# Two transposed token tiles in two pairs of banks, a first gated chunk cut by token tile, and a weight split moved between two additions

## The chip, the cores and the metric

One core of a Trainium2 chip runs one program; everything is fp32 in and out. The metric is the device time of one execution in microseconds, lower is better. Matmuls run on the tensor engine (TensorE, PE) and write to PSUM; VectorE (DVE), ScalarE (ACT) and GpSimd (POOL) do the rest, SyncE (SP) starts the weight loads.

## What is computed

Two transformer blocks, one behind the other, on one sequence of 256 tokens of 1024 features. The change touches the first:

```python
def first_block(x, ...):
    for i in range(DEPTH):                      # 2 layers
        h = rms_norm(x, ln_attn_g[i])
        dq, dk, dv, mq, mk, mv = jnp.split(h @ w_in[i], cuts, axis=-1)
        ...                                     # two kinds of attention, causal
        x = x + jnp.concatenate([y_diff, y_moba], axis=-1) @ w_out[i]
        x = x + conv_ffn(rms_norm(x, ln_ffn_g[i]), w_up[i], conv_w[i], conv_b[i], w_down[i])
    return x

def conv_ffn(h, w_up, conv_w, conv_b, w_down):
    u = causal_dwconv(h @ w_up, conv_w, conv_b)
    g, up = jnp.split(u, 2, axis=-1)            # 2816 features each
    return (jax.nn.silu(g) * up) @ w_down
```

The second block (modulated norms, a recurrent mixer, three more attentions, squared-relu MLPs) begins with norms of a context (`mix_ctx`) and of the stream (`mix_lat`), whose products (`projA`) follow the last `down1`.

## The kernel before

**Products.** Each large product is a sum of three rounded (single-pass) matmuls per k-tile of 128: the operands are split into a rounded high half and a rounded rest, and `mm3` (L401 to L403) multiplies high by high, high by low and low by high. Weights come in chunks of 128 x 2048 numbers (1 MB), loaded by SyncE into 4 raw slots. ScalarE writes a chunk's high half (`ahead_act`, L374), VectorE subtracts it in place (`ahead_dve`, L385, "the split"). Both work in chunk order up to HIGH = 3 chunks ahead of the product. A token product (`tok_gemm`: `qkv`, `out1`, `down1`) keeps 128 tokens as the stationary side and moves 512 weight columns; it works in blocks of 512 columns, in each in pieces of 4 k-tiles, in each piece first token tile 0, then tile 1. `out1` has 2 pieces a block, `down1` 6, of which the last has 2 k-tiles. The gated product (`up1_pe`, L1353) is by features: the stationary side is a tile of 128 weight columns, the moving side all 256 tokens, in 22 chunks; each fills one accumulation bank with 2 (gate and up) x 256 tokens, in 2 x 8 x 3 = 48 matmuls.

**Banks.** PSUM has 8 banks: 4 `acc`, 2 `tr` for transposes, 2 `sc` for scores. Every fill has a number within its pool, fixed ahead by `stage`; `claim` waits until the bank's former fill has been drained, `filled` until the fill is there, `drain` counts a drained one.

**The residual and the norm.** Both products that end a half layer are added to the stream by VectorE in `add_dve` (L1338): for each block of 512 columns the splits that fall due, then the additions of token tile 0 and tile 1 (L1345), then the last split. Then the norm follows, by 128-token tile: ScalarE squares and sums (`norm_square`, L582), GpSimd adds epsilon and takes the power -0.5 (L589, L591), VectorE scales the tile (`norm_scale`, L602), TensorE transposes it in two halves of 4 blocks of 128x128 (`norm_turn`, L611), ScalarE writes the rounded high half with the gain (`norm_high`, L638), VectorE the low half (`norm_low`, L656). The norms with a shift (second block) use L628, L634, L648 and L653 in their place. `norm_dve` (L659) sets VectorE's order: scale tile 0, low half of tile 0's first half, scale tile 1, the other three low halves. Both tiles' four halves go through the 2 `tr` banks, so tile 1's transposes wait until tile 0's banks are drained.

**What follows the norms.** `qkv_pe` (attention, layer 1) starts with tile 0's first half, turns tile 1 after 12 matmuls, and takes tile 0's second half before tile 1. `up1_pe` waits in its first chunk for both tiles' halves (L1361, `norm_ready` L673). After the last `down1` `projA_pe` starts with the context and turns the stream's tiles after its first and second feature tile (L725), so the stream's norm is wanted later there.

The order of work on each engine is the order in which the code is written; nothing reorders it.

Of the kernel before, what the change touches and what calls it, by code (L numbers as in the profile page):

```python
# [11 lines left out]
ALU = mybir.AluOpType  # L12
# [115 lines left out]
def first_and_second_block(nc, I, consts, out):  # L128

    with ExitStack() as ctx:  # L130
# [279 lines left out]
        norm_n = {}  # L410

        def plan_norm(key):
            norm_n[key] = len(norm_n)
            stage(("norm", key), tr=4)

# [157 lines left out]
        def norm_fill(key, tt, half):  # L573

            return tr_at[("norm", key)] + 2 * tt + half

# [16 lines left out]
        def norm_scale(dve, norm, tt):  # L593

            key, src, ready, gain, shift, dst = norm
            n = norm_tile(key, tt)
            ready(dve, tt)
            if norm_n[key]:
                before = [k for k in norm_n if norm_n[k] == norm_n[key] - 1][0]
                dve.wait_ge(tr_full, norm_fill(before, tt, 1) + 1)  # L600
            dve.wait_ge(norm_rstd, n + 1)
            dve.tensor_scalar(xn[:, tt, :], src[:, tt, :], norm_rs[:, n:n + 1], None, ALU.mult).then_inc(norm_xn, 1)  # L602

        def norm_turn(pe, key, tt):

            pe.wait_ge(norm_xn, norm_tile(key, tt) + 1)
            for half in range(2):
                ps = claim(pe, "tr", norm_fill(key, tt, half))
# [3 lines left out]
                ins.then_inc(tr_full, 1)  # L612

# [7 lines left out]
        def norm_high(act, norm, tt):  # L621

            key, src, ready, gain, shift, dst = norm
            if shift:
                f, hi, lo, cols = norm_quarter(norm, tt, 1)
                ps = filled(act, "tr", f)
                for k, (kt, c) in enumerate(cols):
                    ins = act.activation(lo[:, k, :], ps[:, c], ACT.Identity, bias=shift(kt), scale=gain(kt))  # L628
                ins.then_inc(drain("tr", f), 1)
            for half in range(2):  # L630
                f, hi, lo, cols = norm_quarter(norm, tt, half)
                if shift:
                    wait_drained(act, "tr", f)
                    ins = act.activation(r32(hi), lo, ACT.Copy)  # L634
                else:
                    ps = filled(act, "tr", f)
                    for k, (kt, c) in enumerate(cols):
                        ins = act.activation(r32(hi[:, k, :]), ps[:, c], ACT.Identity, scale=gain(kt))  # L638
                ins.then_inc(norm_high_set, 1)

        def norm_low(dve, norm, tt, half):
# [3 lines left out]
            if shift and half == 0:  # L645
                ps = filled(dve, "tr", f)
                for k, (kt, c) in enumerate(cols):
                    ins = dve.tensor_scalar(lo[:, k, :], ps[:, c], gain(kt), shift(kt), ALU.mult, ALU.add)  # L648
                ins.then_inc(drain("tr", f), 1)
            dve.wait_ge(norm_high_set, 2 * norm_tile(key, tt) + half + 1)  # L650
            if shift:
                wait_drained(dve, "tr", f)
                dve.tensor_tensor(r32(lo), lo, r32(hi), ALU.subtract).then_inc(mod_norm_done, 1)  # L653
            else:
                for k, (kt, c) in enumerate(cols):
                    ins = dve.scalar_tensor_tensor(r32(lo[:, k, :]), bank("tr", f)[:, c], gain(kt), r32(hi[:, k, :]), ALU.mult, ALU.subtract)  # L656
                ins.then_inc(drain("tr", f), 1)

        def norm_dve(dve, *norms, scaled=0):  # L659

            for n, norm in enumerate(norms):
                if n >= scaled:
                    norm_scale(dve, norm, 0)
                if not norm[4]:
                    norm_low(dve, norm, 0, 0)
                if n >= scaled:
                    norm_scale(dve, norm, 1)
                for tt in range(TT):
                    for half in range(2):
                        if norm[4] or tt or half:  # L670
                            norm_low(dve, norm, tt, half)

        def norm_ready(pe, key, tt, half):  # L673
# [4 lines left out]
            else:  # L678
                wait_drained(pe, "tr", norm_fill(key, tt, half))

# [669 lines left out]

# [3 lines left out]
        def up1_pe(pe, l):  # L1354
            for i in range(FT):
                w = parts(pe, chunk_at[("up1", l)] + i)
                f = acc_at[("up1", l)] + i
                ps = claim(pe, "acc", f)
                for s in range(2):
                    for kt in range(KT):  # L1360
                        if i == 0 and s == 0 and kt % 4 == 0:  # L1361
                            for tt in range(TT):
                                norm_ready(pe, ("ffn", l), tt, kt // 4)
                        ins = mm3(pe, ps[:, s * SEQ:(s + 1) * SEQ], both(w, lambda v: v[:, kt, s, :]), both(hT, lambda v: v[:, kt, :]),
                                  kt == 0, kt == KT - 1)
                ins.then_inc(acc_full, 1)
# [1760 lines left out]
```

## Time and profile before

| | |
|---|---|
| runs shown | 2091.50, 2093.78, 2087.97 us; median 2091.5 |
| profiled execution | 2088.72 us; span of the profile 2086.9 us |
| TensorE matmul busy | 1930.2 us, 92% of the span, 15696 matmuls |
| VectorE busy | 1132.6 us, 54% |
| ScalarE busy | 868.3 us, 42% |
| GpSimd busy | 223.4 us, 11% |
| mean granted clock of TensorE | 0.963 |
| transposes of the norms | L611, 176 matmuls, 32.6 us busy, 45.4 us idle before them, most of it for L602 |

The profile is of one execution. A duration of a matmul includes its way through the pipeline, so the price of one in a row of them is the distance between starts. A granted clock of 1.00 is full speed and 0.50 the half.

### The profile page before, as it was taken

The page shows a single profiled execution, that of the slowest core. Times are in us where ns is not written, and L with a number is a line of the kernel's source. Part 1 is how long each engine was busy: PE and PEld are TensorE (multiplying, and loading weights), DVE is VectorE, ACT ScalarE, POOL GpSimd, SP SyncE. Part 2 cuts the span into 40 slices and gives each one's busy share as a digit, 9 for nine tenths or more (in the row PEclk, how much of TensorE's full clock was granted, in tenths as well). Part 3 has the DMA queues.
Part 4 walks back from the last instruction along what each step waited for, and adds up shares of the span by engine and source line. Part 5 has one row for each costly group of instructions (what it writes and reads, how often), then busy time and mean ns, then how long its engine had stood idle before and what let it go on. Part 6 is the DMA issues. An engine that isn't in the chain of part 4 may idle for free. (4 is left out here: it accounts for less than half of the span.)

```text
span 2086.9 us, 36823 instructions
## 1 busy us (share of the span) xinstructions
PE 1930.2 (92%) x15696; PEld 1612.7 (77%) x15696; DVE 1132.6 (54%) x1790; ACT 868.3 (42%) x1539; POOL 223.4 (11%) x257
## 2 busy tenths in 40 slices
PE   5997999899899999989999998899999979888998
PEld 4746998685699878856888887688888668577986
DVE  4565675465567655456556565444344445436643
ACT  4344564345456543445322234322232243545532
POOL 1100122020012200101212211200000011000000
PEclk9998999999899999999999998999999999998999
DMA  7574565468456542235000031523233214014653
GB/s 251 176 274 139 162 184 181 141 199 304 141 151 189 176 153 90 91 127 162 24 4 3 4 124 59 137 86 98 84 101 96 67 61 131 31 41 129 192 185 121
DMA packets 231610, 264.54 MB, mean 127 GB/s; under 512 B 14182, under 2 KB 153750, under 8 KB 231063
## 3 DMA queue, kind: packets, MB, share of 16 engines
q1 hardware_dynamic: 222023, 259.23, 39.0%
q10 hardware_dynamic: 9424, 2.95, 0.8%
q8 instruction: 125, 2.05, 0.4%
q14 instruction: 38, 0.31, 0.1%
HBM read 261.07 MB, written 1.09 MB: 126 GB/s over the span
## 5 line engine op out<-in xcount | busy, mean ns | idle before, releaser
L401 PE MATMUL acc<-rounded,rounded 128*128 128x512 f32 (+1 forms) x2552 | 880.9, 345 | 33.2 <-DVE rounded L653 11.0
L402 PE MATMUL acc<-rounded,rounded 128*128 128x512 f32 (+1 forms) x2552 | 874.8, 343 | 0.0
L403 PE MATMUL acc<-rounded,rounded 128*128 128x512 f32 (+1 forms) x2552 | 874.0, 342 | 0.0
L385 DVE TENSOR_TENSOR rounded<-arena,rounded 128x2048 fp32r<-128x2048 f32 (+1 forms) x194 | 435.0, 2246 | 298.6 <-ACT rounded L374 298.5
L401 PEld LDWEIGHTS acc<-rounded,rounded 128*128 128x128 f32 x2552 | 488.0, 191 | 102.4 <-issue 28.8
L403 PEld LDWEIGHTS acc<-rounded,rounded 128*128 128x128 f32 x2552 | 487.3, 191 | 60.7
L402 PEld LDWEIGHTS acc<-rounded,rounded 128*128 128x128 f32 x2552 | 488.1, 191 | 59.3 <-issue 0.2
L374 ACT ACTIVATE rounded<-arena 128x2048 fp32r<-128x2048 f32 (+1 forms) x194 | 362.8, 1872 | 357.8 <-PE acc L403 321.0
L1982 PE MATMUL sc<-arena 64*64 64x64 f32 x2560 | 98.9, 225 | 14.3 <-DVE arena L2128 12.7
L1982 PEld LDWEIGHTS sc<-arena 64*64 64x64 f32 x2560 | 87.1, 138 | 24.1 <-DVE arena L2128 15.8
L1399 DVE SCALAR_TENSOR_TENSOR arena<-acc,pcol,arena 128x254 f32<-128x254 f32 (+1 forms) x176 | 76.8, 478 | 51.2 <-ACT arena L1380 49.7
L2517 ACT ACTIVATE arena<-acc 128x512 f32<-128x512 f32 (+1 forms) x64 | 31.3, 491 | 167.5 <-PE acc L403 143.7
L823 PEld LDWEIGHTS sc<-arena 128*128 128x128 f32 x592 | 72.3, 194 | 36.4 <-ACT arena L929 22.1
L2531 DVE TENSOR_TENSOR arena<-arena 128x512 f32<-128x512 f32 (+1 forms) x64 | 37.4, 585 | 110.0 <-ACT arena L2517 110.0
L1982 PE MATMUL acc<-arena 64*64 64x64 f32 (+1 forms) x2496 | 91.7, 229 | 2.2 <-issue 0.8
L1982 PEld LDWEIGHTS acc<-arena 64*64 64x64 f32 x2496 | 88.0, 134 | 4.9 <-issue 3.3
L914 ACT ACTIVATE arena<-acc,stat 128x256 f32<-128x256 f32 (+2 forms) x128 | 66.2, 524 | 57.2 <-DVE stat L856 32.0
L823 PE MATMUL sc<-arena 128*128 128x64 f32 (+1 forms) x592 | 81.8, 285 | 7.7 <-ACT arena L929 7.4
L1380 ACT ACTIVATE arena<-acc,pcol 128x256 f32<-128x256 f32 x88 | 44.9, 560 | 105.3 <-PE acc L403 105.3
L2380 POOL TENSOR_TENSOR stat<-stat,half 128x1 f32<-128x1 f32 x12 | 8.7, 728 | 657.7 <-DVE stat L2495 657.7
L611 PE MATMUL tr<-keep,arena 128*128 128x128 f32 x176 | 32.6, 339 | 45.4 <-DVE arena L602 34.5
L2438 DVE TENSOR_TENSOR arena<-arena,acc 128x512 f32<-128x512 f32 x56 | 37.9, 685 | 67.2 <-PE acc L403 67.2
(244 smaller groups left out, 1709.3 us busy)
## 6 DMA issues: line engine op xcount, KB each, us to landing
arena<-in_w_ff SPq DMA_DIRECT2D x64, 1024.0 KB, 5.4
arena<-in_w_ada SPq DMA_DIRECT2D x48, 1024.0 KB, 5.2
arena<-in_w_up SPq DMA_DIRECT2D x88, 512.0 KB, 5.1
arena<-in_w_in SPq DMA_DIRECT2D x24, 1024.0 KB, 5.2
arena<-in_w_down SPq DMA_DIRECT2D x20, 1024.0 KB, 5.1
arena<-in_w_out SPq DMA_DIRECT2D x16, 1024.0 KB, 5.2
arena<-in_w_in_even SPq DMA_DIRECT2D x9, 1024.0 KB, 5.4
arena<-in_w_in_odd SPq DMA_DIRECT2D x8, 1024.0 KB, 5.2
```

Of the source, the lines that this page charges most:

```text
L374: act.activation(r32(high_slot(c)[:, 0:size(c)]), raw_slot(c)[:, 0:size(c)], ACT.Copy).then_inc(high_made, 1)
L385: dve.tensor_tensor(r32(w), w, r32(high_slot(c)[:, 0:size(c)]), ALU.subtract).then_inc(split_made, 1)
L401: pe.matmul(ps, ah, bh, start=first, stop=False)
L402: pe.matmul(ps, ah, bl, start=False, stop=False)
L403: return pe.matmul(ps, al, bh, start=False, stop=last)
L823: ins = pe.matmul(ps[:, m * e:(m + 1) * e], self.probT[:, u % 2, n * P:(n + 1) * P], x, start=(kb == 0), stop=(kb == self.width(u) // P - 1))
L914: act.activation(self.prob[:, u % 2, m, 0:w], bank("acc", f)[:, 0:w], ACT.Exp, bias=self.neg_max[:, 2 * u + m:2 * u + m + 1], accum_out=se ...
L1380: act.activation(conv[:, i % 2, s, :], ps[:, s * SEQ:(s + 1) * SEQ], ACT.Identity, bias=col("conv_b", l * 2 * FT + s * FT + i), scale=conv ...
L1399: ins = dve.scalar_tensor_tensor(c, ps[:, s * SEQ:(s + 1) * SEQ - back], conv_col(l, j, i, s), c, ALU.mult, ALU.add)
L1982: ins = pe.matmul(out[h], lhsT[h], rhs[h], start=start, stop=stop)
L2438: ins = dve.tensor_tensor(o, o, ps[:, :], ALU.add)
L2531: dve.tensor_tensor(lo, lo, lo, ALU.mult).then_inc(hid_squared, 1)
```

## The change

`two_pools` names three norms: attention of layer 1, and ffn of both layers. For these, tile 1 is transposed into the 2 `sc` banks and tile 0 into the 2 `tr` banks, VectorE scales both tiles before any low half, and everything that drains a tile asks `norm_fill` for pool and number. In the first of the 22 gated chunks the 256 tokens are cut in two blocks of 128, each with all its matmuls, the second behind the first, and each waits only for its own tile: 96 matmuls of 128 columns in place of 48 of 256. In `add_dve`, for the second block of columns, the last of the splits that stood ahead of both additions stands between them (in both `out1` and both `down1`).

```diff
+        def two_pools(key):
+            return key in (("attn", 1), ("ffn", 0), ("ffn", 1))
         def plan_norm(key):
             norm_n[key] = len(norm_n)
-            stage(("norm", key), tr=4)
+            stage(("norm", key), tr=2, sc=2) if two_pools(key) else stage(("norm", key), tr=4)
...
         def norm_fill(key, tt, half):
-            return tr_at[("norm", key)] + 2 * tt + half
+            if two_pools(key) and tt:
+                return "sc", sc_at[("norm", key)] + half
+            return "tr", tr_at[("norm", key)] + 2 * tt + half
...
         def norm_dve(dve, *norms, scaled=0):
             for n, norm in enumerate(norms):
                 if n >= scaled:
                     norm_scale(dve, norm, 0)
-                if not norm[4]:
+                early = not norm[4] and not two_pools(norm[0])
+                if early:
                     norm_low(dve, norm, 0, 0)
                 if n >= scaled:
                     norm_scale(dve, norm, 1)
                 for tt in range(TT):
                     for half in range(2):
-                        if norm[4] or tt or half:
+                        if not early or tt or half:
                             norm_low(dve, norm, tt, half)
...
         def add_dve(dve, key, kts, after=None):
-            def add(hf):
+            g, n = chunk_at[key], -(-kts // 4)
+            for hf in range(2):
+                for i in range(n - 1 - hf):
+                    ahead_dve(dve, g + n * hf + i + HIGH)
                 for tt in range(TT):
                     f = acc_at[key] + 2 * hf + tt
                     ps = filled(dve, "acc", f)
                     x = h_lat[:, tt, hf * 512:(hf + 1) * 512]
                     dve.tensor_tensor(x, x, ps[:, :], ALU.add).then_inc(drain("acc", f), 1)
+                    if hf and tt == 0:
+                        ahead_dve(dve, g + 2 * n - 2 + HIGH)
                 if after:
                     after(hf)
-            tok_walk(dve, ahead_dve, key, kts, 2, add, last=False)
+                if not hf:
+                    ahead_dve(dve, g + n - 1 + HIGH)
...
         def up1_pe(pe, l):
...
-                for s in range(2):
-                    for kt in range(KT):
-                        if i == 0 and s == 0 and kt % 4 == 0:
-                            for tt in range(TT):
-                                norm_ready(pe, ("ffn", l), tt, kt // 4)
-                        ins = mm3(pe, ps[:, s * SEQ:(s + 1) * SEQ], both(w, lambda v: v[:, kt, s, :]), both(hT, lambda v: v[:, kt, :]),
-                                  kt == 0, kt == KT - 1)
+                for t0, t1 in ([(0, P), (P, SEQ)] if i == 0 else [(0, SEQ)]):
+                    for s in range(2):
+                        for kt in range(KT):
+                            if i == 0 and s == 0 and kt % 4 == 0:
+                                norm_ready(pe, ("ffn", l), t0 // P, kt // 4)
+                            ins = mm3(pe, ps[:, s * SEQ + t0:s * SEQ + t1], both(w, lambda v: v[:, kt, s, :]),
+                                      both(hT, lambda v: v[:, kt, t0:t1]), kt == 0, kt == KT - 1)
```

How the order moves. VectorE at the end of `out1` of layer 0 and through the norm, before (L385 the splits, L1345 the additions, L602 the scalings, L656 the low halves, 4 instructions to a half):

```order
L385 TENSOR_TENSOR rounded_69<-arena,rounded_64 128x2048
L385 TENSOR_TENSOR rounded_66<-arena,rounded_65 128x2048
L1345 TENSOR_TENSOR h_lat<-h_lat,acc 128x512 x2
L602 TENSOR_SCALAR arena<-h_lat,stat 128x1024
L656 SCALAR_TENSOR_TENSOR rounded_52<-tr,pcol,rounded_51 128x128 x4
L602 TENSOR_SCALAR arena<-h_lat,stat 128x1024
L656 SCALAR_TENSOR_TENSOR rounded_52<-tr,pcol,rounded_51 128x128 x12
```

and with the change (the additions are L1360 there, the scalings L612, the low halves L667):

```order
L385 TENSOR_TENSOR rounded_69<-arena,rounded_64 128x2048
L1360 TENSOR_TENSOR h_lat<-h_lat,acc 128x512
L385 TENSOR_TENSOR rounded_66<-arena,rounded_65 128x2048
L1360 TENSOR_TENSOR h_lat<-h_lat,acc 128x512
L612 TENSOR_SCALAR arena<-h_lat,stat 128x1024 x2
L667 SCALAR_TENSOR_TENSOR rounded_52<-tr,pcol,rounded_51 128x128 x8
L667 SCALAR_TENSOR_TENSOR rounded_52<-sc,pcol,rounded_51 128x128 x8
```

The second split has moved behind the first addition, and the second scaling ahead of all low halves; the same holds at `out1` of layer 1 and `down1` of layer 0.

TensorE where the norm meets the gated product in layer 0, before (L611 the transposes, L401 to L403 the three matmuls of a k-tile):

```order
L611 MATMUL tr<-keep,arena 128x128 x16
L401 MATMUL acc<-rounded_51,rounded_64 128x256
L402 MATMUL acc<-rounded_52,rounded_64 128x256
L403 MATMUL acc<-rounded_51,rounded_69 128x256
L401 MATMUL acc<-rounded_51,rounded_64 128x256
```

and with the change (transposes L622):

```order
L622 MATMUL tr<-keep,arena 128x128 x8
L622 MATMUL sc<-keep,arena 128x128 x8
L401 MATMUL acc<-rounded_51,rounded_64 128x128
L402 MATMUL acc<-rounded_52,rounded_64 128x128
L403 MATMUL acc<-rounded_51,rounded_69 128x128
L401 MATMUL acc<-rounded_51,rounded_64 128x128
```

The second 8 transposes go to the score banks, and the first chunk's matmuls have half the columns and twice the number. VectorE behind the last `down1`, before:

```order
L385 TENSOR_TENSOR rounded_69<-arena,rounded_64 128x2048
L385 TENSOR_TENSOR rounded_66<-arena,rounded_65 128x2048
L1345 TENSOR_TENSOR h_lat<-h_lat,acc 128x512 x2
L602 TENSOR_SCALAR arena<-h_lat,stat 128x1024 x2
L648 TENSOR_SCALAR arena<-tr,mod_gain,mod 128x128 x4
```

and with the change:

```order
L385 TENSOR_TENSOR rounded_69<-arena,rounded_64 128x2048
L1360 TENSOR_TENSOR h_lat<-h_lat,acc 128x512
L385 TENSOR_TENSOR rounded_66<-arena,rounded_65 128x2048
L1360 TENSOR_TENSOR h_lat<-h_lat,acc 128x512
L612 TENSOR_SCALAR arena<-h_lat,stat 128x1024 x2
```

Here only the split has moved; the norm's own order is what it was.

## Rows read from the trace of the kernel before

**Rows 1.** TensorE's waits: line, line waited for: us in total, times, longest
```profile
PE tr L611 <- DVE arena L602: 34.5, 10, 7.2
...
PE tr L1009 <- DMA arena<-in_c_ctx: 8.6, 1, 8.6
```
**Rows 2.** Timeline, VectorE, end of out1 and norm, layer 0: start, us, instruction [idle before]
```profile
193.68 2.29 DVE L385 TENSOR_TENSOR rounded<-arena,rounded 128x2048 fp32r<-128x2048 f32 x1 [3.31 <-ACT rounded L374]
195.88 0.68 DVE L1345 TENSOR_TENSOR h_lat<-h_lat,acc 128x512 f32<-128x512 f32 x1
197.26 0.69 DVE L1345 TENSOR_TENSOR h_lat<-h_lat,acc 128x512 f32<-128x512 f32 x1 [0.70 <-PE acc L403]
198.93 0.75 DVE L602 TENSOR_SCALAR arena<-h_lat,stat 128x1024 f32<-128x1024 f32 x1 [0.98 <-POOL stat L591]
201.61 1.13 DVE L656 SCALAR_TENSOR_TENSOR rounded<-tr,pcol,rounded 128x128 fp32r<-128x128 f32 x4 [1.93 <-ACT rounded L638]
202.66 0.74 DVE L602 TENSOR_SCALAR arena<-h_lat,stat 128x1024 f32<-128x1024 f32 x1
```
**Rows 3.** Timeline, ScalarE, the same norm and the first gated chunks
```profile
196.68 1.06 ACT L582 ACTIVATE arena<-h_lat 128x1024 f32<-128x1024 f32 x1 [3.04 <-DVE h_lat L1345]
...
200.44 2.17 ACT L638 ACTIVATE rounded<-tr,pcol 128x128 fp32r<-128x128 f32 x8 [1.22 <-PE tr L611]
...
214.71 1.02 ACT L1380 ACTIVATE arena<-acc,pcol 128x256 f32<-128x256 f32 x2 [6.12 <-PE acc L403]
...
220.39 1.02 ACT L1380 ACTIVATE arena<-acc,pcol 128x256 f32<-128x256 f32 x2 [2.85 <-PE acc L403]
```
**Rows 4.** Timeline, TensorE, the same norm and first chunk; last row layer 1
```profile
199.74 1.19 PE L611 MATMUL tr<-keep,arena 128*128 128x128 f32 x8 [2.52 <-DVE arena L602]
203.46 2.15 PE L611 MATMUL tr<-keep,arena 128*128 128x128 f32 x8 [2.53 <-DVE arena L602]
207.05 0.55 PE L401 MATMUL acc<-rounded,rounded 128*128 128x256 f32 x1 [1.44 <-DVE rounded L656]
...
210.60 0.40 PE L402 MATMUL acc<-rounded,rounded 128*128 128x256 f32 x1
...
575.73 0.55 PE L401 MATMUL acc<-rounded,rounded 128*128 128x256 f32 x1 [1.45 <-DVE rounded L656]
```
**Rows 5.** Stretches: length, busy us (x count) of PE, PEld, DVE, ACT, POOL, clock, DMA share, GB/s
```profile
180.00:194.00 14.00, 14.00 (x61) 11.24 (x60) 6.19 (x5) 5.75 (x3) 0.00 (x0) 1.00 0.62 170
774.00:777.40 3.40, 3.40 (x19) 3.40 (x18) 2.36 (x6) 2.54 (x6) 0.00 (x0) 0.51 0.00 0
```
**Rows 6.** Timeline, end of down1 and attention norm of layer 1: VectorE, then TensorE
```profile
394.79 2.29 DVE L385 TENSOR_TENSOR rounded<-arena,rounded 128x2048 fp32r<-128x2048 f32 x1 [3.31 <-ACT rounded L374]
397.00 1.28 DVE L1345 TENSOR_TENSOR h_lat<-h_lat,acc 128x512 f32<-128x512 f32 x2
400.04 0.76 DVE L602 TENSOR_SCALAR arena<-h_lat,stat 128x1024 f32<-128x1024 f32 x1 [1.76 <-POOL stat L591]
...
400.85 1.97 PE L611 MATMUL tr<-keep,arena 128*128 128x128 f32 x8 [5.31 <-DVE arena L602]
404.36 0.80 PE L401 MATMUL acc<-rounded,rounded 128*128 128x512 f32 x1 [1.54 <-DVE rounded L656]
```
**Rows 7.** Timeline behind the last down1: VectorE, then TensorE
```profile
766.65 2.29 DVE L385 TENSOR_TENSOR rounded<-arena,rounded 128x2048 fp32r<-128x2048 f32 x1 [3.31 <-ACT rounded L374]
...
772.25 0.75 DVE L602 TENSOR_SCALAR arena<-h_lat,stat 128x1024 f32<-128x1024 f32 x1 [2.11 <-POOL stat L591]
...
773.06 1.09 PE L611 MATMUL tr<-keep,arena 128*128 128x128 f32 x8 [2.81 <-DVE arena L602]
```
**Rows 8.** Timeline, TensorE: rows of short matmuls at full clock (attention, transposes)
```profile
123.32 0.71 PE L823 MATMUL sc<-arena 128*128 128x128 f32 x4
123.87 0.95 PE L1121 MATMUL tr<-keep,arena 128*128 128x2 f32 x8
...
778.35 1.04 PE L611 MATMUL tr<-keep,arena 128*128 128x128 f32 x8
```
**Rows 9.** Groups by line and shape, TensorE: out<-in, shapes, count, busy us, mean ns
```profile
L401 PE MATMUL acc<-rounded,rounded 128*128 128x512 f32 x1304 | 523.6, 402 | 16.5 <-ACT arena L2517 5.5 <-DVE rounded L1330 3.1 <-DVE arena L2436 3.0
...
L401 PE MATMUL acc<-rounded,rounded 128*128 128x256 f32 x1248 | 357.3, 286 | 16.8 <-DVE rounded L653 11.0 <-DVE rounded L656 2.9 <-ACT arena L2693 2.6
```

More of the change, by code:

```diff
@@ L573, in norm_fill, with norm_turned @@
         def norm_fill(key, tt, half):
-            return tr_at[("norm", key)] + 2 * tt + half
+            if two_pools(key) and tt:
+                return "sc", sc_at[("norm", key)] + half
+            return "tr", tr_at[("norm", key)] + 2 * tt + half
+        def norm_turned(eng, key, tt):
+            pool, f = norm_fill(key, tt, 1)
+            eng.wait_ge(POOLS[pool][1], f + 1)
         def norm_square(act, norm, tt):
@@ L599, in norm_scale @@
                 before = [k for k in norm_n if norm_n[k] == norm_n[key] - 1][0]
-                dve.wait_ge(tr_full, norm_fill(before, tt, 1) + 1)
+                norm_turned(dve, before, tt)
             dve.wait_ge(norm_rstd, n + 1)
@@ L607, in norm_turn @@
             for half in range(2):
-                ps = claim(pe, "tr", norm_fill(key, tt, half))
+                pool, f = norm_fill(key, tt, half)
+                ps = claim(pe, pool, f)
                 for k in range(4):
@@ L611, in norm_turn @@
                     ins = pe.transpose(ps[:, k * P:(k + 1) * P], xn[:, tt, kt * P:(kt + 1) * P], ident)
-                ins.then_inc(tr_full, 1)
+                ins.then_inc(POOLS[pool][1], 1)
         def norm_quarter(norm, tt, half):
@@ L625, in norm_high @@
                 f, hi, lo, cols = norm_quarter(norm, tt, 1)
-                ps = filled(act, "tr", f)
+                ps = filled(act, *f)
                 for k, (kt, c) in enumerate(cols):
                     ins = act.activation(lo[:, k, :], ps[:, c], ACT.Identity, bias=shift(kt), scale=gain(kt))
-                ins.then_inc(drain("tr", f), 1)
+                ins.then_inc(drain(*f), 1)
             for half in range(2):
@@ L632, in norm_high @@
                 if shift:
-                    wait_drained(act, "tr", f)
+                    wait_drained(act, *f)
                     ins = act.activation(r32(hi), lo, ACT.Copy)
                 else:
-                    ps = filled(act, "tr", f)
+                    ps = filled(act, *f)
                     for k, (kt, c) in enumerate(cols):
@@ L645, in norm_low @@
             if shift and half == 0:
-                ps = filled(dve, "tr", f)
+                ps = filled(dve, *f)
                 for k, (kt, c) in enumerate(cols):
                     ins = dve.tensor_scalar(lo[:, k, :], ps[:, c], gain(kt), shift(kt), ALU.mult, ALU.add)
-                ins.then_inc(drain("tr", f), 1)
+                ins.then_inc(drain(*f), 1)
             dve.wait_ge(norm_high_set, 2 * norm_tile(key, tt) + half + 1)
             if shift:
-                wait_drained(dve, "tr", f)
+                wait_drained(dve, *f)
                 dve.tensor_tensor(r32(lo), lo, r32(hi), ALU.subtract).then_inc(mod_norm_done, 1)
@@ L655, in norm_low @@
                 for k, (kt, c) in enumerate(cols):
-                    ins = dve.scalar_tensor_tensor(r32(lo[:, k, :]), bank("tr", f)[:, c], gain(kt), r32(hi[:, k, :]), ALU.mult, ALU.subtract)
-                ins.then_inc(drain("tr", f), 1)
+                    ins = dve.scalar_tensor_tensor(r32(lo[:, k, :]), bank(*f)[:, c], gain(kt), r32(hi[:, k, :]), ALU.mult, ALU.subtract)
+                ins.then_inc(drain(*f), 1)
         def norm_dve(dve, *norms, scaled=0):
@@ L678, in norm_ready @@
             else:
-                wait_drained(pe, "tr", norm_fill(key, tt, half))
+                wait_drained(pe, *norm_fill(key, tt, half))
         def tok_gemm(pe, key, f, kts, blocks, lhsT, ready=None, before=None, pieces=None):
```

## The prediction

> **What bounds the kernel now.** First the page's busy times (table above): TensorE is busy 92% of the span, so only its idle time, its time at the low clock, and matmuls added to it can move the end. Then TensorE's waits over the whole run [rows 1]: the largest is the transposes of the norms (L611) waiting for the scaled tile (L602), 34.5 us in 10 waits; the only transfer that it waits for comes at the very start. Then the timelines at the four places that the change reaches, read engine by engine. In the vector engine's timeline at the end of out1 of layer 0 [rows 2], the reader is to see a queue: a weight split L385 of 2.29 us stands ahead of both additions L1345; the scaling L602 of the second tile (202.66) waits behind the low halves L656 of the first (201.61), and these behind the scalar engine's high halves, made from 200.44 on [rows 3]. TensorE [rows 4] stands still 2.52 us, turns tile 0, stands 2.53 us, turns tile 1 (203.46) and starts the gated chunk at 207.05 at the low clock: 16 steps of 128x256 in 3.55 us up to 210.60, the first 0.35, the others 0.21 each. The next chunk, at the high clock, takes from evacuation to evacuation 220.39 - 214.71 = 5.68 us for 48 steps [rows 3], 0.118 each. These are the 1.2 and the 2.4 GHz level. Layer 1 repeats this: its gated chunk starts at 575.73 [rows 4].
>
> Against all this the sum is made on the profiled execution, 2088.7 us; the median of the runs shown is 2091.5, 2.8 above it, and I carry the difference over to that median. About 0.3%, 6.3 us, is what a measurement of this kernel can tell from no change.
>
> **Part 1: the split between the two additions.** It only reorders the vector engine. In out1's second half tile 0 is complete when the 12 matmuls of tile 1 begin, 12 x 0.233 = 2.8 us (60 steps of 512 columns in 14 us [rows 5]) before the end of the product at 199.74 - 2.52 = 197.22 [rows 4], so at about 194.5; its addition ran at 195.88 because L385 stood ahead. It now runs at 194.5 to 195.2, L385 to 197.5, and tile 1's addition at 197.5, 0.25 later than before. After down1 of layers 0 and 1 the last piece has two k-tiles, so tile 0 is complete 6 x 0.233 = 1.4 us before the end, and the same happens there. The split's own user, the second chunk of the next product, is more than 2.8 us away, so its 0.1 to 0.3 us of delay is worth nothing.
>
> **Part 2: attention norm of layer 1.** TensorE ended down1 at 400.85 - 5.31 = 395.54 [rows 6]. Tile 0 is complete at 394.15; both additions stood behind L385 (394.79), which waited for the high split. Now: addition 394.2 to 394.9, square and reciprocal root 1.15 + 0.96 us (their sum is at most what lies between 196.68 and the scaling at 198.93 [rows 2, 3]), ready at 397.1; L385 to 397.2, second addition to 397.85, scaling 0.75 to 398.6. It ended at 400.80. So tile 0 is turned 2.2 us earlier. The first low halves no longer stand ahead of tile 1's scaling: that one waits for its own root, to 400.2, and ends at 401.0, just when the first high half is made (turn start + 1.15 + 1.1 = 400.95), so the low halves cost nothing more. The product begins at 402.2 instead of 404.36: **-2.2 us**. Tile 1 is turned inside that product as before; the other bank pair changes nothing there, since it was not waited for.
>
> **Part 3: the norm after the last down1** (not one of the three). The vector engine's queue is the same: L385 at 766.65 to 768.94, both additions behind it, scaling at 772.25 [rows 7]. TensorE works through the context's first feature tile until 770.25 and then waits 2.81 us for the scaling. With the split between the additions tile 0 is added at 766.1, rooted at 769.0, scaled behind the second addition at 769.75 to 770.5: the wait shrinks to about 0.3, a gain of 2.5. And the low clock that followed it, 3.4 us at 0.51 [rows 5], in which 16 steps took 0.21 instead of 0.118, has no idle time left to cause it: 1.5 more. **-4.0 us**, between -2.5 (the clock falls all the same) and -4.2.
>
> **Part 4: the ffn norms, twice.** Addition of tile 0 195.2, scaling behind the second addition at 198.2 to 198.95: transposes at 199.0 instead of 199.74. Tile 1's square ends 0.3 later than before (199.45), its root at 200.65, its scaling at 201.45, now ahead of all low halves: transposes at 201.5 instead of 203.46, into free score banks, without the 0.3 us that they stood for a turn bank. The low halves of tile 0 run 201.45 to 203.7, those of tile 1 to 206. The gated chunk's first block needs only tile 0: it starts at about 202.9, **4.15 us earlier** than 207.05. Tile 1's halves are done 2 to 3 us before the second block wants them.
>
> Against that stands the chunk's own price: 48 matmuls of 256 columns become 96 of 128. No row has a rounded matmul of 128 columns. Nearest rows [rows 8]: plain f32 with 128 columns, 4 in 0.71 us (0.71 - 0.38)/3 = 0.11 a step; transposes of 128 columns, 8 in 1.04, (1.04 - 0.28)/7 = 0.11; and even with 2 columns, 8 in 0.95, (0.95 - 0.25)/7 = 0.10. What all share is a weight load of 128 columns each, and two columns are no cheaper than 128: a step is held up by its load. So halving the columns halves nothing. I take 0.11, bounds 0.10 (two columns) and 0.118 (the 256-column step itself). With 3.7 us of low clock at double price, a chunk of n steps takes n x s + 1.85 us. Before: 48 x 0.118 + 1.85 = 7.5, which with 0.15 of pipeline gives the evacuation L1380 at 214.71 [rows 3]. After: 96 x 0.11 + 1.85 = 12.4, end at 202.9 + 12.4 + 0.15 = 215.45: **+0.75 us** a layer, bounds -0.2 and +1.5. All 4.15 us won at the start are spent on the extra 48 loads. The Trainium skill (TensorE: Matmul & The Clock Gate, Back-to-back issue gap) gives about 81 ns for a sustained pair of load and 128-column matmul; by it the chunk would take 9.6 us and each layer would gain 2.0. The rows here are all slower than that, and they decide.
>
> **Sum.** -2.2 - 4.0 + 2 x 0.75 = -4.7, at the bounds -2.2 - 4.2 - 0.4 = -6.8 and -2.1 - 2.5 + 3.0 = -1.6. Behind each place the next stage is bound by TensorE, and no transfer holds it [rows 1], so the shift carries to the end: 2084.0 for the profiled execution, **2087** against the median.
>
> **Rivals.**
> 1. *The chunk gets cheap* (faster by more than 0.3%). If the clock does not fall at the ffn norms, or comes back at once, because the two pauses shrink from 2.5 and 2.5 to 1.8 and 1.1 us, each chunk saves its 1.85: 215.45 becomes 213.6, -1.1 a layer, sum -2.2 - 4.0 - 2.2 = -8.4, or 2083. For: the pauses are shorter. Against: the 1.19 us of transposes between two pauses did not keep the clock up [rows 4], and this pattern stays. Chance 0.20. The Trainium skill's 81 ns (page and section named above) points the same way; by it the sum would be about -10.
> 2. *Short rounded matmuls lose their rate* (slower). All 7656 rounded matmuls here have 256 or 512 columns (3 lines of 1304 and 1248 [rows 9]); should the array treat one of 128 like a far longer one, say at the 0.233 of 512 columns, the chunk takes 96 x 0.233 + 1.85 = 24.2, ends at 227.3, +12.5 a layer, sum +18.8, 2110. It decides from the step where 2 x 96 x (s - 0.11) exceeds 6.3 + 4.7, s = 0.167. For: no row excludes it. Against: plain f32 of the same shape takes 0.11. Chance 0.07.
> 3. *The early tiles aren't used.* The low clock comes back after the down1 norm, the short step costs 0.118, or the vector engine, which now waits for tile 1's root before any low half, delays the first half: about -1.6 down to 0, 2090 to 2091.5. The first scaling already waits 0.98 us for its root [rows 2], which speaks for it. Chance 0.13.
>
> **How the numbers follow.** Forecast 0.60 (its own range 2083 to 2091), rivals 0.20, 0.07, 0.13. Faster by over 0.3% needs 2085.2 or less: rival 1 and the lower edge of the forecast, 0.25. Slower: rival 2 and a little, 0.08. Same: 0.67. The range takes rival 1 at its far end and rival 3 with 2 to 3 us for the spread of the runs, 2080 to 2094.5; rival 2 is left out.
>
> **What would show it.** After: additions of tile 0 ahead of L385 at four ends of products; the wait of the transposes on L602 down by about 2 at layer 1's attention, 2.5 before the second block and 2 to 3 at each ffn norm; the gated chunk's first matmul 4 us earlier and its evacuation 0.75 later. Wrong if the 128-column step is not 0.10 to 0.118, if the granted clock behind the last down1 still falls, or if a new wait appears on the first low half.

## The result, and the profile after

| | before | after |
|---|---|---|
| median | 2091.26 us (4 runs, 2087.97 to 2093.78) | 2114.57 us (4 runs, 2112.02 to 2120.54) |
| ratio | | 1.0112, 95% interval 1.0088 to 1.0135 |
| profiled execution | 2088.72 us | 2120.54 us |
| TensorE matmul busy | 1930.2 us | 1975.2 us, 15792 matmuls |
| mean granted clock | 0.963 | 0.947 |

The change makes the kernel 23 us slower. TensorE has 96 matmuls more and is busy 45 us longer, while it waits less for the scalings: the group in [rows 1] fell from 34.5 to 26.0 us (24.0 in turns into `tr`, 2.0 in turns into `sc`). So the loss isn't a wait. The timeline of the first changed place, layer 0's norm, VectorE and then TensorE, in the profile after (start, us, instruction, idle before it):

```profile
198.96 0.69 DVE L1360 TENSOR_TENSOR h_lat<-h_lat,acc 128x512 f32<-128x512 f32 x1 [4.10 <-PE acc L403]
199.57 2.29 DVE L385 TENSOR_TENSOR rounded<-arena,rounded 128x2048 fp32r<-128x2048 f32 x1
201.77 0.68 DVE L1360 TENSOR_TENSOR h_lat<-h_lat,acc 128x512 f32<-128x512 f32 x1
202.73 0.75 DVE L612 TENSOR_SCALAR arena<-h_lat,stat 128x1024 f32<-128x1024 f32 x1 [0.28 <-POOL stat L601]
204.82 0.75 DVE L612 TENSOR_SCALAR arena<-h_lat,stat 128x1024 f32<-128x1024 f32 x1 [1.34 <-POOL stat L601]
...
201.33 0.39 PE L403 MATMUL acc<-rounded,rounded 128*128 128x512 f32 x1
203.54 1.09 PE L622 MATMUL tr<-keep,arena 128*128 128x128 f32 x8 [1.82 <-DVE arena L612]
205.63 1.97 PE L622 MATMUL sc<-keep,arena 128*128 128x128 f32 x8 [1.00 <-DVE arena L612]
207.25 0.45 PE L401 MATMUL acc<-rounded,rounded 128*128 128x128 f32 x1
```

Everything up to the chunk came out as argued: the split stands between the additions, both scalings stand ahead of the low halves, the pauses are 1.8 and 1.0 us instead of 2.52 and 2.53 [rows 4]. out1 ends at 201.72 and the chunk begins 5.5 us later, where it was 207.05 - 197.22 = 9.8. Its price did not come out. ScalarE's evacuations of the first two gated chunks, and TensorE's stretches (length, busy us and count of PE, PEld, DVE, ACT, POOL, clock, DMA share, GB/s), both after:

```profile
228.01 1.02 ACT L1397 ACTIVATE arena<-acc,pcol 128x256 f32<-128x256 f32 x2 [17.26 <-PE acc L403]
235.87 1.02 ACT L1397 ACTIVATE arena<-acc,pcol 128x256 f32<-128x256 f32 x2 [5.04 <-PE acc L403]
```

```profile
204.00:206.00 2.00, 1.00 (x8) 0.77 (x7) 1.18 (x3) 1.77 (x8) 0.60 (x2) 0.82 1.16 328
206.00:210.00 4.00, 4.00 (x21) 4.00 (x20) 3.69 (x15) 3.62 (x11) 0.00 (x0) 0.50 0.18 44
...
220.00:225.00 5.00, 5.00 (x26) 5.00 (x25) 0.00 (x0) 0.00 (x0) 0.00 (x0) 0.50 0.01 3
...
228.00:232.00 4.00, 4.00 (x20) 4.00 (x20) 2.89 (x5) 2.82 (x3) 0.00 (x0) 0.50 0.72 206
232.00:233.00 1.00, 1.00 (x8) 1.00 (x8) 1.00 (x1) 0.00 (x0) 0.00 (x0) 0.70 0.87 221
233.00:236.00 3.00, 3.00 (x27) 3.00 (x27) 0.15 (x1) 0.14 (x1) 0.00 (x0) 1.00 0.01 3
```

The clock falls in the second pause (its mean over 205 to 206 is 0.65); before the change it fell at the end of the first turn (0.81 over 200 to 201). What differs is the return. TensorE works without a gap at 0.50, the 1.2 GHz level, through the whole cut chunk (20.76 us for 96 matmuls, 0.213 a step) and some 4 us into the next one, whose 256-column matmuls see it return. In layer 1 it is the same: low from 587.6 to 614.9, where the chunk's evacuation comes at 610.28 (such moments are worked out here from the mean clock of 1 us stretches). The account of a layer, from out1's end to the second evacuation: start 4.3 earlier; chunk 20.76 instead of 214.71 - 207.05 = 7.66, +13.1; next chunk 7.86 instead of 5.68, +2.2; together 34.1 instead of 23.2, **+11.0**. Layer 1 gives the same: out1's end at 585.80 - 1.81 = 583.99, second evacuation at 618.16, 34.2.

The other two places gained what was forecast. Layer 1's attention norm, then the norm behind the last down1 with the clock of its stretch, after:

```profile
414.24 1.97 PE L622 MATMUL tr<-keep,arena 128*128 128x128 f32 x8 [3.21 <-DVE arena L612]
417.74 0.80 PE L401 MATMUL acc<-rounded,rounded 128*128 128x512 f32 x1 [1.54 <-DVE rounded L667]
...
800.06 1.10 PE L622 MATMUL tr<-keep,arena 128*128 128x128 f32 x8 [0.73 <-DVE arena L612]
803.84 1.04 PE L622 MATMUL tr<-keep,arena 128*128 128x128 f32 x8
```

```profile
800.00:805.00 5.00, 4.94 (x43) 4.94 (x44) 3.32 (x9) 2.75 (x7) 0.77 (x2) 1.00 0.30 95
```

down1 ended at 414.24 - 3.21 = 411.03 and the next product begins 6.7 us later instead of 8.8 [rows 6]: -2.1. From layer 1's second gated evacuation to the last turn it is 803.84 - 618.16 = 185.7 instead of 778.35 - 589.05 = 189.3: -3.6, and the clock of 0.51 that stood there [rows 5] is 1.00. The changed places sum to 2 x 11.0 - 2.1 - 3.6 = +16.3. The two profiled executions differ by 31.8. The other 15.5 lies in code that did not change: 4.5 before the end of layer 0's out1 (201.72 against 197.22), 4.7 between layer 1's attention norm and its out1 (clock 0.70 over the last 50 us there, against 0.84 over the last 46 before), 6.3 behind the last down1. The first two are for the most part a low clock as well. TensorE in layer 0's attention, a row and a stretch of each, after and then before:

```profile
157.22 1.94 PE L1119 MATMUL sc<-arena,silu_c 128*32 128x512 f32 x8
160.00:180.00 20.00, 17.02 (x70) 13.46 (x71) 10.45 (x15) 9.43 (x10) 0.00 (x0) 0.50 0.30 106
...
156.84 1.06 PE L1107 MATMUL sc<-arena,silu_c 128*32 128x512 f32 x8
160.00:180.00 20.00, 15.09 (x72) 11.77 (x72) 11.35 (x13) 9.43 (x10) 0.00 (x0) 0.74 0.28 101
```

In both the clock has fallen by 151. Before, it is back at 156.2 and low once more from 166.5 to 176.7. After, it stays low from 150.7 to 181.4, though TensorE works without a gap from 150.4 to 170.3. Up to the row of eight at 152.3 the two keep step; at out1's first matmul they are 4.35 us apart (177.16 against 172.81). In layer 1 the clock stays low from 533.0 to 563.7, where before it was back from 524.9 to 535.1; that is 3.8 of the 4.7. In layer 0 nothing that the change touches has run by then. Of the profiles below, those of cut_again and pools_alone have such stretches of 30.7 us in both layers and five more have one in layer 1, with and without a cut; whether the change makes them likelier isn't shown. The medians differ by 23.3, in the repeat below by 17.5.

### The profile page after: what moved, and what is told of

The parts are those of the page before. It is cut to its first block and busy times, and to the rows that moved or that the text cites. A ratio compares the mean times of both kernels' runs of the same rounds, so it can differ in the third digit from the quotient of the medians.

```text
span 2118.7 us, 37011 instructions
## 1 busy us (share of the span) xinstructions
PE 1975.2 (93%) x15792; PEld 1652.6 (78%) x15792; DVE 1132.1 (53%) x1790; ACT 868.6 (41%) x1539; POOL 224.3 (11%) x257
## 3 DMA queue, kind: packets, MB, share of 16 engines
HBM read 261.07 MB, written 1.09 MB: 124 GB/s over the span
## 5 line engine op out<-in xcount | busy, mean ns | idle before, releaser
L401 PE MATMUL acc<-rounded,rounded 128*128 128x512 f32 (+2 forms) x2584 | 900.2, 348 | 30.7 <-DVE rounded L664 11.0
L402 PE MATMUL acc<-rounded,rounded 128*128 128x512 f32 (+2 forms) x2584 | 894.3, 346 | 0.0
L403 PE MATMUL acc<-rounded,rounded 128*128 128x512 f32 (+2 forms) x2584 | 893.9, 346 | 0.0
L385 DVE TENSOR_TENSOR rounded<-arena,rounded 128x2048 fp32r<-128x2048 f32 (+1 forms) x194 | 435.0, 2246 | 289.1 <-ACT rounded L374 289.0
L401 PEld LDWEIGHTS acc<-rounded,rounded 128*128 128x128 f32 x2584 | 504.7, 195 | 99.4 <-issue 25.6
L403 PEld LDWEIGHTS acc<-rounded,rounded 128*128 128x128 f32 x2584 | 504.0, 195 | 60.9
L402 PEld LDWEIGHTS acc<-rounded,rounded 128*128 128x128 f32 x2584 | 504.6, 195 | 59.1 <-issue 0.2
L816 PE MATMUL acc<-arena 64*128 64x256 f32 (+2 forms) x256 | 61.1, 536 | 11.2 <-ACT arena L926 10.7
```

The costliest lines, as they stand in the source:

```text
L385: dve.tensor_tensor(r32(w), w, r32(high_slot(c)[:, 0:size(c)]), ALU.subtract).then_inc(split_made, 1)
L401: pe.matmul(ps, ah, bh, start=first, stop=False)
L402: pe.matmul(ps, ah, bl, start=False, stop=False)
L403: return pe.matmul(ps, al, bh, start=False, stop=last)
L816: pe.matmul(ps[:, 0:self.width(u)], self.q(u, m), self.k(u, m), start=True, stop=True).then_inc(acc_full, 1)
```

## The experiments

One theory (A) runs through the expectations: the cut costs twice as many steps, each at 0.11 or 0.21 us by the clock, and a clock that is low when the 128-column matmuls begin stays low as long as they last. The rival (B): these matmuls themselves pull the clock down, or are slow, wherever they stand. Each batch ran beside its own runs of before (medians 2092.5, 2092.6 and 2093.1).

| run | median us (runs) | ratio to before, 95% |
|---|---|---|
| wide | 2079.35 (12) | 0.9953, 0.9932 to 0.9975 |
| cut_tenth | 2094.32 (10) | 1.0028, 1.0003 to 1.0052 |
| cut_alone | 2120.88 (4) | 1.0146, 1.0116 to 1.0177 |
| half_cut | 2089.76 (10) | 0.9990, 0.9965 to 1.0015 |
| cut_again | 2110.09 (4) | 1.0090, 1.0064 to 1.0116 |
| split_alone | 2085.14 (12) | 0.9973, 0.9960 to 0.9987 |
| pools_alone | 2091.89 (12) | 0.9996, 0.9973 to 1.0019 |
| cut_filled | 2092.91 (10) | 1.0006, 0.9989 to 1.0024 |
| wide_filled | 2084.03 (12) | 0.9970, 0.9950 to 0.9991 |
| cut_short_fill | 2086.62 (12) | 0.9968, 0.9949 to 0.9988 |
| wide_short_fill | 2075.36 (6) | 0.9913, 0.9883 to 0.9944 |

**wide: the change without the cut.**

```diff
-                for t0, t1 in ([(0, P), (P, SEQ)] if i == 0 else [(0, SEQ)]):
+                for t0, t1 in [(0, SEQ)]:
...
```

The chunk waits for both tiles again.

> The change without the cut: the first gated chunk keeps 48 matmuls of 256 columns; the two pairs of banks and the moved split stay. Theory A (the clock does not come back while TensorE runs matmuls of 128 columns, and the cut alone costs): all of the loss goes and the three other gains stay. Attention norm -2.1, the norm behind the last down1 -4, ffn norms about -1.3 a layer (in the changed kernel the last low half ends 8.4 us after out1, before the chunk began 9.8 after it): 2091 - 9 = 2082. Rival C (banks or order of the norms cost): it stays above 2100.

It beats both kernels, before by 13 us. Its clock falls at the same place as the changed kernel's. TensorE's timeline with the first evacuation, and its stretches:

```profile
202.23 1.97 PE L622 MATMUL sc<-keep,arena 128*128 128x128 f32 x8 [1.00 <-DVE arena L612]
205.83 0.55 PE L401 MATMUL acc<-rounded,rounded 128*128 128x256 f32 x1 [1.63 <-DVE rounded L667]
...
213.22 1.02 ACT L1398 ACTIVATE arena<-acc,pcol 128x256 f32<-128x256 f32 x2 [5.87 <-PE acc L403]
```

```profile
208.00:209.00 1.00, 1.00 (x7) 1.00 (x7) 1.00 (x1) 0.00 (x0) 0.00 (x0) 0.50 0.00 0
209.00:210.00 1.00, 1.00 (x10) 1.00 (x10) 0.67 (x1) 0.00 (x0) 0.00 (x0) 0.97 0.00 0
```

The pauses up to the second turn are the same (1.81 and 1.00), and there is one of 1.63 more, yet the clock is back 3.2 us into the 256-column matmuls. Only the width of what follows differs. The other profiles say the same: in both layers of before, wide, cut_tenth, split_alone and pools_alone, ten uncut chunks that began at the low clock, it was back 3.0 to 6.0 us after the first matmul; in both layers of after, cut_alone and cut_again, six cut ones, it never came back within the chunk.

**cut_tenth: the same cut, in the eleventh chunk instead of the first.** There TensorE comes from 256-column matmuls at the high clock.

```diff
-                for t0, t1 in ([(0, P), (P, SEQ)] if i == 0 else [(0, SEQ)]):
+                for t0, t1 in ([(0, P), (P, SEQ)] if i == 10 else [(0, SEQ)]):
...
```

> The changed kernel with the chunk number 10 cut by token tile in place of the first, so that the 96 matmuls of 128 columns begin at the high clock. Theory A: at the high clock a step takes 0.11 us (held up by its weight load), 10.6 us a chunk for 5.7, so +5 a layer over the kernel without a cut, 2092, if the high clock holds; if narrow matmuls also let it fall, steps of 0.21 begin at some point inside the chunk, with the granted clock at 0.5 from there. Rival B (a rounded matmul of 128 columns has lost its rate, whatever the clock): steps of 0.21 from the first one, with the granted clock still at 1.00, +15 a layer, 2112.

TensorE's first cut steps, the evacuations around the chunk, and the chunk's stretches:

```profile
261.12 0.27 PE L402 MATMUL acc<-rounded,rounded 128*128 128x128 f32 x1
261.23 0.27 PE L403 MATMUL acc<-rounded,rounded 128*128 128x128 f32 x1
261.34 0.28 PE L401 MATMUL acc<-rounded,rounded 128*128 128x128 f32 x1
...
261.26 1.02 ACT L1398 ACTIVATE arena<-acc,pcol 128x256 f32<-128x256 f32 x2 [2.24 <-PE acc L403]
271.93 1.02 ACT L1398 ACTIVATE arena<-acc,pcol 128x256 f32<-128x256 f32 x2 [7.23 <-PE acc L403]
```

```profile
261.00:266.00 5.00, 5.00 (x47) 5.00 (x47) 3.36 (x6) 3.43 (x5) 1.43 (x2) 1.00 0.76 206
266.00:272.00 6.00, 6.00 (x55) 6.00 (x55) 1.02 (x1) 0.07 (x1) 0.00 (x0) 1.00 0.02 4
```

96 steps take 10.67 us, 0.111 each, and the clock stays at 1.00 throughout, in layer 1 too (645.57 - 634.90). So B is out: the cut matmuls have the rate that was forecast and don't bring the clock down. The cut's bare price is 10.67 - 5.68 = 5.0 us a layer, 10 in all; the run is 15.0 above wide, and its ten runs spread from 2091.56 to 2109.77, so some 5 us more are in the medians than the chunk shows. Where they lie isn't shown; a low clock in the attention, as in its own profile from 518.0 to 548.7, is one candidate.

**cut_alone: before, with the cut and nothing else.** The diff is the last hunk of the change.

> The kernel before with nothing but the cut of the first gated chunk. Theory A: the chunk starts when tile 1 is turned, about 1.4 us earlier than before, takes 96 x 0.213 = 20.5 us instead of 7.5, and the next chunk pays about 2 us for the return of the clock: +13.5 a layer, 2118, more than the whole change, whose other parts gain. Rival C: less than half of the loss, under 2103.

The loss is there without any other part. In its profile the two pauses are the old ones, the chunk's evacuation comes at 222.71 and the next at 229.30, with the clock at 0.50 until the cut matmuls are done. From out1's end to the second evacuation that is 35.4 us, +12.2 a layer where 13.5 was expected:

```profile
203.00:222.00 19.00, 19.00 (x91) 19.00 (x91) 3.93 (x8) 2.29 (x3) 0.00 (x0) 0.50 0.00 1
```

**half_cut: only the gate half of the first chunk cut,** the up half whole.

```diff
-                for t0, t1 in ([(0, P), (P, SEQ)] if i == 0 else [(0, SEQ)]):
-                    for s in range(2):
+                for s in range(2):
+                    for t0, t1 in ([(0, P), (P, SEQ)] if i == 0 and s == 0 else [(0, SEQ)]):
```

> The changed kernel with only the gate half (s = 0) of the first chunk cut by token tile, the other half in matmuls of 256 columns: 48 narrow and 24 wide ones. Theory A: 48 x 0.213 = 10.2 us at the low clock, then the clock comes back some 4 us into the wide ones, 4.6 us: 14.9 us for the chunk, against 20.5 for the full cut and 7.5 for none; the next chunk pays nothing. With the start 3 us earlier than without a cut this is +4.4 a layer over it, 2091. Rival B (the step's price, not the clock): the same narrow part, but the clock comes back inside it.

It doesn't show what half the narrow matmuls cost at the low clock, and shows something else. Its runs lie in two groups, three at 2078.6 to 2079.2 and seven at 2087.0 to 2096.3, and the profiled execution is of the first: the same pauses, but the clock never fell.

```profile
201.53 1.09 PE L622 MATMUL tr<-keep,arena 128*128 128x128 f32 x8 [1.80 <-DVE arena L612]
203.63 1.09 PE L622 MATMUL sc<-keep,arena 128*128 128x128 f32 x8 [1.00 <-DVE arena L612]
...
200.00:205.00 5.00, 2.44 (x19) 2.00 (x19) 3.38 (x9) 3.92 (x13) 1.38 (x3) 1.00 0.75 210
```

The second turn takes 1.09 us here, in both layers, and 1.97 in after and wide. In layer 0 the program is theirs up to this point, so whether pauses of 1.8 and 1.0 us bring the clock down is not fixed by the program; it can differ between executions. That the upper group are executions in which it fell is likely (2091 was expected for them), but only the profiled one was seen.

**cut_again: the changed kernel once more,** unedited.

> The changed kernel once more, for more executions: does the clock fall at the ffn norms every time? Theory A, always: all runs 2110 to 2121. If in some executions it holds, as in the profile of the kernel with half the cut, those runs come some 10 us lower a layer, down to 2095.

The loss repeats at 17.5 us, near the 16.3 of the account above. Two of the four runs, 2103.0 and 2109.0, lie below the 2110 that A had for each; whether the clock held at one of their norms was not seen. The picture of the profiled run (2114.75) repeats as well: evacuations at 225.67 and 233.51, the clock 0.50 over the whole stretch from 205 to 225.

```profile
205.00:225.00 20.00, 20.00 (x97) 20.00 (x95) 4.75 (x11) 3.41 (x8) 0.00 (x0) 0.50 0.00 1
```

**split_alone and pools_alone: one part of the gain each.** The first is before with the new `add_dve`, the second is wide with the old one.

> The kernel before with nothing but the moved split. By my steps: attention norm -2, behind the last down1 -4 (wait 2.8 to 0.7 us and the clock stays up), ffn norms -0.7 each for the earlier first tile, less what the low halves still hold up: 2092 - 6 = 2086. Rival: the split only matters together with the two bank pairs: no change.

> The two pools for the three norms and the scalings ahead of the low halves, without the cut and without the moved split. The moved split alone measured 2085.1 against 2092.6 before, the two together without the cut 2079.4. If the two parts add up, this one gives the rest of the gain, some 6 us below before: 2085 to 2088. By the trace, scalings of tile 1 come 1.3 us sooner at each ffn norm (2 x 1.3 = 2.6) and at the attention norm tile 0's scaling is not earlier, so the expectation by my steps is -2 to -4: 2088 to 2090. Rival: the parts overlap, the split alone gives all, and this one is at 2092.

The moved split alone brings 7.5 us, the pools 1.2, which is no measured difference. At the ffn norm of layer 0 the profiles give, from out1's end to the first gated matmul, 9.8 before, 9.1 with the split, 7.7 with the pools and 7.5 with both. TensorE in the three runs (split_alone, pools_alone, and the first turn of wide):

```profile
197.61 1.09 PE L611 MATMUL tr<-keep,arena 128*128 128x128 f32 x8 [1.81 <-DVE arena L602]
...
204.92 0.55 PE L401 MATMUL acc<-rounded,rounded 128*128 128x256 f32 x1 [1.45 <-DVE rounded L656]
```

```profile
204.16 1.10 PE L622 MATMUL tr<-keep,arena 128*128 128x128 f32 x8 [2.51 <-DVE arena L612]
...
209.39 0.55 PE L401 MATMUL acc<-rounded,rounded 128*128 128x256 f32 x1 [1.63 <-DVE rounded L667]
```

```profile
200.13 1.10 PE L622 MATMUL tr<-keep,arena 128*128 128x128 f32 x8 [1.81 <-DVE arena L612]
```

For the split: 2 x 0.7 at the ffn norms, 2.1 at the attention norm and about 4 behind the last down1, 7.5, as measured. For the pools: 2 x 2.1 = 4.2 by the trace, 1.2 measured, within its interval (-5.6 to +4.0). Both together would be 7.5 + 2 x (9.1 - 7.5) = 10.7; wide measured 13.2, also within its interval (-14.2 to -5.2).

**cut_filled and wide_filled: TensorE kept at work in the pauses.** Plain fp32 matmuls into the idle accumulation bank: 9 ahead of the first turn, 5 ahead of the second, and in wide 7 ahead of the first gated matmul.

```diff
                 for tt in range(TT):
+                    ps = claim(pe, "acc", acc_at[("up1", l)])
+                    for _ in range(9 if tt == 0 else 5):
+                        pe.matmul(ps[:, 0:256], ident, keep[:, 0:256], start=True, stop=True)
                     norm_turn(pe, ("ffn", l), tt)
```

> The changed kernel, cut and all, with dummy matmuls (f32, 256 columns, of constants into the accumulation bank that the first gated chunk claims and overwrites) in TensorE's two pauses at the ffn norms: 9 before tile 0 is turned, 5 before tile 1. They are extra work that the result does not use. Theory A (the loss is the clock, not the cut as such): the clock stays high into the gated chunk, whose 96 matmuls then take 96 x 0.111 = 10.7 us instead of 20.5, and the next chunk pays nothing: -12 a layer against the changed kernel, about 2090 to 2080. Rival B2 (narrow matmuls at that place are slow for another cause, the banks or the operands of the norm): still 2110 or more.

> The kernel without the cut, with dummy matmuls in all three pauses at the ffn norms (9, 5, and 7 between the second turn and the gated chunk). They are extra work that the result does not use. Theory A: 3.7 us at half the clock a layer are saved, and the transposes run at full speed: -2 to -2.7 a layer, 2075; the fillers may hold a ready transpose up by 0.2. Rival: the fillers cost what they save, 2080.

The cut kernel comes down by 17 to 22 us, and in its profile the clock is 1.00 through both norms, so the pauses are where the loss begins. But A's numbers were missed: 2092.9 where it had 2080 to 2090, and 2084.0 where it had 2075 and the rival 2080. The filler was too long. In the profile of wide_filled:

```profile
199.87 4.05 PE L3026 MATMUL acc<-keep 128*128 128x256 f32 x18
203.75 1.04 PE L622 MATMUL tr<-keep,arena 128*128 128x128 f32 x8
```

One such matmul counts as two records and takes 0.45 us; nine of them fill 4.05 us of a 1.8 us pause and push the turn back. (One of cut_filled's ten runs took 3795.7 us, for a reason that isn't known; the ratio leaves it out.)

**cut_short_fill and wide_short_fill: the same, no longer than the pauses.** 4 and 2 such matmuls, and in wide 3 more.

```diff
-                    for _ in range(9 if tt == 0 else 5):
+                    for _ in range(4 if tt == 0 else 2):
```

> The changed kernel with 4 and 2 plain fp32 matmuls of 256 columns in the first two pauses at each ffn norm, 1.8 and 0.9 us, no longer than the pauses; the third pause, before the first gated matmul, is not filled. Theory A: the clock stays at 1.00, so each of the two cut chunks takes 10.7 us instead of 20.5 and the next one 5.7 instead of 7.9; start unchanged: about 2087 to 2090, 8 above the kernel without the cut. Rival (the clock falls all the same, from the unfilled third pause): 2110 to 2117, as the change itself.

> The kernel without the cut, with 4, 2 and 3 plain fp32 matmuls of 256 columns into the idle accumulation bank in the pauses of 1.8, 1.0 and 1.6 us at each ffn norm (one took 0.45 us in the earlier filled runs, so 1.8, 0.9 and 1.35 us: no longer than the pauses). Theory A (the low clock follows the idle time at the norm): with the pauses filled and nothing pushed back the clock is 1.00 through both norms, which is worth up to 1.85 us a layer in the executions in which it would have fallen: 2076 to 2079 against 2079.4 of the same kernel unfilled. Rival (filler costs what it saves): 2082 to 2085, as with the longer filling (2084.0).

Both came out as A has it. The cut chunk of cut_short_fill, TensorE, ScalarE and stretch:

```profile
199.75 1.09 PE L622 MATMUL sc<-keep,arena 128*128 128x128 f32 x8
200.88 0.30 PE L401 MATMUL acc<-rounded,rounded 128*128 128x128 f32 x1
...
211.82 1.02 ACT L1397 ACTIVATE arena<-acc,pcol 128x256 f32<-128x256 f32 x2 [7.40 <-PE acc L403]
217.56 1.02 ACT L1397 ACTIVATE arena<-acc,pcol 128x256 f32<-128x256 f32 x2 [2.90 <-PE acc L403]
...
205.00:210.00 5.00, 5.00 (x47) 5.00 (x46) 1.75 (x1) 0.00 (x0) 0.00 (x0) 1.00 0.02 3
```

The same cut kernel, with six small idle matmuls a layer added, is 24 to 28 us faster than without them. Its 96 matmuls have the place, the banks and the operands of those in the change, so none of these makes them slow. And wide_short_fill, at 2075.4, has the lowest median, 18 us below before; its interval overlaps that of wide:

```profile
199.45 1.10 PE L622 MATMUL sc<-keep,arena 128*128 128x128 f32 x8
200.38 1.46 PE L3029 MATMUL acc<-keep 128*128 128x256 f32 x6
202.64 0.36 PE L401 MATMUL acc<-rounded,rounded 128*128 128x256 f32 x1 [0.80 <-DVE rounded L667]
...
208.60 1.02 ACT L1398 ACTIVATE arena<-acc,pcol 128x256 f32<-128x256 f32 x2 [4.47 <-PE acc L403]
```

out1's last matmul is followed by filler at 195.68 in the first profile and at 195.38 in the second. Counted from there the uncut chunk starts later and ends sooner: even at the high clock the cut buys 2.1 us of start (7.26 - 5.20) for 5.0 of steps, 2.9 a layer. The two profiled executions differ by 3.9, the medians by 11.3, where these are 5.9; the rest was not traced.

## Why the prediction was wrong

Forecast 2087, within 0.3% of before; measured 2114.6, slower by 1.1%, outside the range.

- **Part 1** held: the additions and splits stand where it put them. That the reorder alone is the largest gain of the change (7.5 us, split_alone) is the sum of what it does in parts 2 to 4.
- **Part 2** held: -2.2 forecast, -2.1 in the trace.
- **Part 3** held: -4.0 forecast, -3.6 in the trace; the wait shrank from 2.81 to 0.73 us (0.3 forecast) and the low clock behind it is gone.
- **Part 4, the start**, held: 4.15 us sooner forecast, 4.3 in the trace.
- **Part 4, the step price**, held: 0.11 us, measured 0.111 at the high clock (cut_tenth). At the low one it is 0.213, outside the 0.10 to 0.118 beyond which the prediction called itself wrong; that is the failure of the next item. Row and rule differed here, and the row was right: the 81 ns that the Trainium skill (TensorE: Matmul & The Clock Gate, Back-to-back issue gap) gives for a sustained pair are shown by no run for these rounded matmuls.
- **Part 4, the formula, is the step that failed**: "with 3.7 us of low clock at double price, a chunk of n steps takes n x s + 1.85 us". The 3.7 us were read from 256-column matmuls [rows 4] and carried over to 128-column ones as if they were a property of the pause. They aren't even fixed at 256 columns (3.0 to 6.0 us in ten chunks), and at 128 columns the low clock did not end within the chunk in any of six: 20.8 us instead of 12.4, and 2.2 more in the next chunk. That is +11.0 a layer where +0.75 was forecast, and 2 x 10.25 = 20.5 of the 27.6 us between forecast and median. The rest wasn't traced in the runs that make the median; in the profiled execution what exceeds the account lies in unchanged code, some 8 of its 15.5 us in two attentions with a longer low clock.

Rival 2 came near in its time (2110) and was wrong in its mechanism: it let the array lose its rate at 128 columns at any clock, and cut_tenth shows the rate is kept. Rival 1 asked the right question, whether the clock falls, and looked only at the side on which it gains. The missing rival was its mirror: the clock falls and does not come back. Its price could be had from the rows: 96 x 0.21 = 20.2 against 7.5 for the chunk, less 4.15 of start, is +8.5 a layer, and with -6.2 elsewhere +10.8 in all, 2102. It lacks the 2.2 us in the next chunk and what the unchanged code adds.

The Trainium skill (TensorE: Matmul & The Clock Gate, Why this matters for your kernels) warns of thin matmuls, that the clock oscillates from k-tile to k-tile unless all k-tiles are done before the next transfer is waited for. The cut chunk does its k-tiles back to back, without a transfer between them. Its clock indeed did not oscillate, but this order did not bring it back up either: it stayed at 0.50 without a break.

What stays open is why these matmuls keep a low clock low. No width between 128 and 256 columns was tried, and no number of cut matmuls but 96 was seen at the low clock. The cut isn't the only thing that keeps it low (the attention above did so for 30.7 us in some executions), and few columns alone don't: in the profile of before the clock fell at 1166.6 and was back at 1170.0 while TensorE did nothing but plain fp32 matmuls of 64 x 64 with 64 columns. Open too is what decides whether the clock falls in pauses of 1.8 and 1.0 us.

## What to carry to other kernels

Price a matmul that follows a pause at the clock that it would find, and don't carry the length of a low-clock stretch from wide matmuls to narrow ones: put narrow rounded ones where the clock is high, or keep it high with filler measured to be no longer than the pause. A rounded matmul of 128 columns stepped at 0.111 us here and one of 256 at 0.118, so halving the moving side doubled the steps and saved almost nothing in each; such a cut must buy more start than it costs (here 2.1 us for 5.0). When a change with several parts loses, run it with each part taken out: here the rest was worth 13 us, and 18 with nine idle matmuls a layer. And before a difference between two profiled executions is put down to the change, subtract what lies in code that both share (here 15.5 of 31.8 us).

## What the runs showed of the hardware that was not expected

- 128-column rounded matmuls, back to back, neither raise a low clock (0.50 for some 20 us in the profiles of after, cut_alone and cut_again, both layers) nor lower a high one (1.00 for 10.7 us in cut_tenth).
- The same pauses of 1.8 and 1.0 us brought the clock down in the profiles of after, cut_again, wide and cut_tenth, and not in that of half_cut, in both layers each time.
- In the same attention code the clock was back after 6.8 us in the profile of before (149.4 to 156.2) and stayed low for 30.7 us in that of after (150.7 to 181.4), with TensorE at work without a gap for the first 20 of them.
- A plain fp32 matmul of 256 columns takes 0.45 us, two records of 0.22, where a rounded one of the same shape takes 0.118.
